# Depthwise convolution taps on VectorE: two operations per tap against one over three blocks of tokens

## The chip, the cores and the metric

The kernel runs on one core of one Trainium2 chip. The metric is device time in microseconds (us) of one execution. Three runs of the kernel before gave 1216.16, 1216.24 and 1216.39 us, median 1216.24. The profile shows one more execution.

## The reference

Two independent groups of tokens pass through two layers with shared weights: 128 context tokens and 256 latent tokens, 384 in all, each 1024 wide. A layer is a mixer part (pooling, two kinds of attention, a Fourier mix, gates, an output projection) and then the part that matters here, a gated MLP with a centred depthwise convolution of width 3 along the tokens of each group:

```
def _conv_ffn(h, w_up, conv_w, conv_b, w_down):
    u = h @ w_up                                   # 1024 -> 5632
    up = jnp.pad(u, ((0, 0), (1, 1), (0, 0)))
    u = up[:, :-2] * conv_w[0] + up[:, 1:-1] * conv_w[1] + up[:, 2:] * conv_w[2] + conv_b
    gate, val = jnp.split(u, 2, axis=-1)
    return (jax.nn.silu(gate) * val) @ w_down      # 2816 -> 1024
```

Every channel adds its left neighbour token times conv_w[0] and its right neighbour times conv_w[2]. Neighbours are taken inside a group alone: token 127 (last of the context) and token 128 (first of the latent group) are not neighbours.

## The kernel before, in words

Channels lie on the 128 partitions and the 384 tokens along the free axis, context in columns 0 to 127 and latent tokens in 128 to 383. `RANGES` is the pair of column ranges (0, 128) and (128, 384).

Weights stream from HBM in units of 128x1024 fp32, through four slots. Each unit is split in two parts: ScalarE copies it to fp32r (`w_hi<-w_raw`), VectorE subtracts that from the original (`w_lo<-w_raw,w_hi`, line 1077), and TensorE multiplies hi by hi, hi by lo and lo by hi (lines 1602 to 1604), 24 matmuls of 384 columns for a unit. TensorE starts a unit only when its w_hi and w_lo are both there (`unit_ready`, lines 1592 to 1595), and a slot is filled again only when TensorE has finished the unit that had it. In program order every engine has its own stream, and the engines meet in semaphores.

The up projection has 44 units in each layer, in pairs of a gate unit and a value unit. I call what VectorE and ScalarE do for one such pair a block: 22 blocks in a layer, numbered from 0. TensorE writes unit n to PSUM bank n modulo 4 in the first layer and modulo 8 in the second. For a block, with m = 0 for the gate and m = 1 for the value unit:

- ScalarE waits for both units, writes the middle tap with bias of each (`mlp_tmp<-bank,params` 128x384, lines 991 to 993), and signals `tap1` after each one.
- VectorE waits for `tap1` of m, adds the left neighbours (line 1492) and the right neighbours (line 1496), each as one operation per range, 127 and 255 columns, with a wait on its own semaphore between the two taps. That makes 8 operations a block. After m = 0 it signals `conv_g`, after m = 1 `conv_v`.
- ScalarE waits for `conv_g`, computes the tanh (`mlp_tmp<-mlp_tmp`), splits a weight unit, waits for `mlp_full`, and writes `mlp_hi`.
- VectorE forms the product (lines 1505 and 1508), splits a weight unit (line 1077), subtracts for `mlp_lo` (line 1080), and in the first layer and later blocks of the second does one row product (line 1108) for the modulation vectors of a later stage. Before the taps it splits another weight unit.

The first four blocks of the second layer differ, because there the up projection begins before the norm is known: VectorE scales the product in its bank (`bank<-bank,rstd`, line 1166, semaphore `rescaled`), ScalarE adds a shift to it in place (`bank<-bank,cond_raw`, 128 and 256 columns) ahead of each middle tap, and both also write normalised activations (`act_hi`, and `act_lo` at line 1144) for the units from 8 on. ScalarE waits there for VectorE's `rescaled` of m = 0 and of m = 1, and VectorE waits for ScalarE's `tap1`.

All ScalarE activations are recorded at line 673, a helper.

Of the kernel before, what the change touches and what calls it, by code (L numbers as in the profile page):

```python
# [19 lines left out]
ACT = mybir.ActivationFunctionType  # L20
ALU = mybir.AluOpType
AX = mybir.AxisListType.X

P = 128
# [5 lines left out]
TOK = CTX + LAT  # L30
# [8 lines left out]
FB = FFN // P  # L39
# [133 lines left out]
def program(nc, stream, start_w, ada_w, ada_rows, start_ada, params, caches, consts, time_consts, x_in, cond,  # L173
            y_out, k_out, v_out, ckv_out, krope_out):
    ctx = ExitStack()
    with ctx:
# [16 lines left out]
        late_t, _ = tile("gated_late", KD * TOK, o)  # L193
# [3 lines left out]
        for s in range(SLOTS):  # L197

            wlo.append(tile(f"w_lo{s}", UNIT, o, F32R)[0])
            t, o = tile(f"w_raw{s}", UNIT, o)  # L200
            raw.append(t)
            t, o = tile(f"w_hi{s}", UNIT, o, F32R)
# [141 lines left out]
        def pc(name, a=0, b=None, p0=0, p1=P):  # L344
            lo, hi = PCOL[name]
            return par[p0:p1, lo + a:(hi if b is None else lo + b)]
# [324 lines left out]
        def _(act):  # L671
            def A(out, in_, func, **kw):
                return nc.scalar.activation(out, in_, func, **kw)  # L673
# [22 lines left out]
            for l in range(DEPTH):  # L696
# [275 lines left out]
                for i in range(FB // 2):  # L972
                    for j in range(2):
                        u = P0 + 2 * j
                        p = l * FB + i * 2 + j
                        f = ftmp[:, j]
                        unnormed = l > 0 and i < 2
                        first, b0 = 3 * (2 * i + j), up_bank(i, 2 * j)
                        if unnormed and p > l * FB:
                            split(u + 4, i)  # L980
                        elif not unnormed and (l == 0 or i > 2 or j > 0):
                            split(u + 3, i)
                        act.wait_ge(unit_done, FROM + l * UNITS + i * SLOTS + u + 2)

                        act.wait_ge(mlp_lo, FROM + l * FB + i * 2 + j)
                        for m in range(2):
                            col = i * 4 + 2 * j + m
                            if unnormed:
                                add_shift(1, b0 + m, bank[b0 + m]).then_inc(shifted, 1)
                                act.wait_ge(shifted, b0 + m + 1)  # L990
                            A(f[:, m, :], bank[b0 + m][:, 0:TOK], ACT.Identity,
                              scale=pc("conv_w", 2 * FB + col, 2 * FB + col + 1),
                              bias=pc("conv_b", col, col + 1)).then_inc(tap1, 1)
                        if unnormed and p == l * FB:
                            split(u + 4, i)
                        if unnormed and first < KD:
                            normed_high(1, first)
                        act.wait_ge(conv_g, FROM + p + 2)
                        A(f[:, 2, :], f[:, 0, :], ACT.Tanh, scale=0.5).then_inc(mlp_tanh, 1)
                        if unnormed and first + 1 < KD:  # L1000
                            normed_high(1, first + 1)
                        split(u + (5 if unnormed else 4), i)
                        act.wait_ge(mlp_full, p + 1)
                        A(ghi[:, i * 2 + j, :], f[:, 3, :],
                          ACT.Copy).then_inc(mlp_hi, 1)
                        if unnormed and first + 2 < KD:
                            normed_high(1, first + 2)
# [27 lines left out]
        def _(dve):  # L1035
# [32 lines left out]
            for l in range(DEPTH):  # L1068
# [406 lines left out]
                for i in range(FB // 2):  # L1475
                    for j in range(2):
                        u = P0 + 2 * j
                        p = l * FB + i * 2 + j
                        f = ftmp[:, j]
                        unnormed = l > 0 and i < 2  # L1480
                        first, b0 = 3 * (2 * i + j), up_bank(i, 2 * j)
                        if unnormed and p > l * FB:
                            split(u + 4, i)
                        elif not unnormed and (l == 0 or i > 2 or j > 0):
                            split(u + 3, i)
                        for m in range(2):
                            dve.wait_ge(tap1, 2 * p + m + 1)
                            b = bank[b0 + m]
                            col = i * 4 + 2 * j + m
                            before, behind = pc("conv_w", col, col + 1), pc("conv_w", 4 * FB + col, 4 * FB + col + 1)  # L1490
                            for a, e, _ in RANGES:
                                own(V.scalar_tensor_tensor(f[:, m, a + 1:e], b[:, a:e - 1], before, f[:, m, a + 1:e],  # L1492
                                                           ALU.mult, ALU.add))
                            own.wait()
                            for a, e, _ in RANGES:
                                ins = V.scalar_tensor_tensor(f[:, m, a:e - 1], b[:, a + 1:e], behind, f[:, m, a:e - 1],  # L1496
                                                             ALU.mult, ALU.add)
                            ins.then_inc((conv_g, conv_v)[m], 1)
                        if unnormed and p == l * FB:
                            split(u + 4, i)  # L1500
                        if unnormed and first < KD:
                            normed_low(1, first)
                        dve.wait_ge(mlp_tanh, p + 1)

                        own(V.scalar_tensor_tensor(f[:, 2, :], f[:, 2, :], 1.0, f[:, 0, :], ALU.add, ALU.mult))
                        own.wait()
                        dve.wait_ge(conv_v, FROM + p + 2)
                        V.scalar_tensor_tensor(f[:, 3, :], f[:, 2, :], 0.5, f[:, 1, :], ALU.mult, ALU.mult).then_inc(mlp_full, 1)
                        if unnormed and first + 1 < KD:
                            normed_low(1, first + 1)  # L1510
                        split(u + (5 if unnormed else 4), i)
                        if unnormed and b0 < FIRST - 2:
                            rescale(1, b0 + 2, bank[b0 + 2][:, 0:TOK])
                        dve.wait_ge(mlp_hi, p + 1)
                        low(glo[:, i * 2 + j, :], f[:, 3, :],
                            ghi[:, i * 2 + j, :]).then_inc(mlp_lo, 1)
                        if unnormed and b0 < FIRST - 2:
                            rescale(1, b0 + 3, bank[b0 + 3][:, 0:TOK])
                        if unnormed and first + 2 < KD:
                            normed_low(1, first + 2)  # L1520
                        if l == 0 or i >= SLOW_ROWS:
                            dve.wait_ge(spread_loaded, 32 + 16 * l)
                            row_products(1, spread, prod_t)
# [664 lines left out]
```

## Time and profile before

| | |
|---|---|
| median of three runs | 1216.24 us |
| the profiled execution | 1215.3 us |
| its span, first to last instruction | 1213.5 us |
| granted TensorE clock | 1.00 throughout |
| busy: TensorE, VectorE, ScalarE, GpSimd | 99%, 78%, 50%, 12% |
| up projection and blocks, first layer | about 353 to 530 us of the span |
| the same, second layer | about 939 to 1127 us |
| line 1492, line 1496 | 64.7 and 65.2 us busy, 176 operations each |
| middle tap on ScalarE | 54.8 us busy, 88 operations |

A row of the timeline reads: start in us of the span, duration in us, engine, line, operation, what is written from what is read, shapes, how many like it were merged (xN), and in brackets how long the engine sat idle before it and what ended that. Where two operations with different numbers of columns are merged (127 and 255), the shape is that of the first. Rows of groups give the number of instructions, total busy time in us, the mean of one in ns, and the idle time before them.

### The profile page before, as it was taken

How to read it: one execution, taken by the hardware profiler on the slowest of the kernel's cores; microseconds unless marked ns; L12 is line 12 of the kernel's file. 1: busy time of each engine (PE TensorE's matmuls, PEld its weight loads, DVE VectorE, ACT ScalarE, POOL GpSimd, SP SyncE). 2: the span in 40 equal slices, each digit the busy share in tenths (PEclk: the TensorE clock that was granted, in tenths of full speed). 3: DMA queues.
4: the chain of work that ended last, by engine and by line, in shares of the span. 5: the costliest groups of instructions: out<-in, count | busy, mean ns of one | idle time of the engine just before them, and what ended most of it. 6: DMA issues, size and time to landing. Idle time of an engine off the chain costs nothing.

```text
span 1213.5 us, 19749 instructions
## 1 busy us (share of the span) xinstructions
PE 1200.7 (99%) x7688; PEld 1146.9 (95%) x7688; DVE 946.2 (78%) x1751; ACT 601.5 (50%) x1023; POOL 149.8 (12%) x125
## 2 busy tenths in 40 slices
PE   8999999999999999999999999999999999999998
PEld 7987999989989999999999889999999999999998
DVE  5587877848689999988867978787687899999432
ACT  3445564543365544543456555646438755454221
POOL 0232000008300000000142500000272200000000
PEclk9999999999999999999999999999999999999999
DMA  9763433544744454457663544343325444454443
GB/s 371 293 223 124 142 119 121 172 142 157 260 175 140 162 168 156 161 197 244 218 249 122 208 139 140 105 133 111 105 87 196 140 134 139 158 167 145 139 139 122
DMA packets 53821, 200.91 MB, mean 166 GB/s; under 512 B 6816, under 2 KB 7232, under 8 KB 51936
## 3 DMA queue, kind: packets, MB, share of 16 engines
q1 hardware_dynamic: 53408, 198.96, 47.9%
q8 instruction: 62, 1.02, 0.3%
q0 software_dynamic: 320, 0.69, 0.2%
q14 instruction: 31, 0.25, 0.1%
HBM read 197.35 MB, written 2.27 MB: 164 GB/s over the span
## 4 chain that ended last, share of the span: by engine, by line
PE 95%; DVE 2%; DMA 1%; issue 1%; SPq 0%; ACT 0%; DVEq 0%
PE bank L1602 28%; PE bank L1604 27%; PE bank L1603 27%; PE bank L1920 1%; PE bank L1900 1%; DMA start_ada<-start_ada 1%; DVE w_lo L1077 1%; PE bank L1669 1%; PE bank L1674 1%; PE bank L1890 1%; PE bank L1673 1%; DVE gated_late L1431 1%; PE bank L1875 1%; PE bank L1658 1%; PE bank L1724 0%
## 5 line engine op out<-in xcount | busy, mean ns | idle before, releaser
L1602 PE MATMUL bank<-act_hi,w_hi 128*128 128x384 f32 x1240 | 421.9, 340 | 0.1
L1604 PE MATMUL bank<-act_hi,w_lo 128*128 128x384 f32 x1240 | 415.0, 335 | 0.0
L1603 PE MATMUL bank<-act_lo,w_hi 128*128 128x384 f32 x1208 | 403.9, 334 | 0.0
L1077 DVE TENSOR_TENSOR w_lo<-w_raw,w_hi 128x1024 fp32r<-128x1024 f32 x251 | 323.5, 1291 | 98.0 <-ACT w_hi L673 97.3
L673 ACT ACTIVATE w_hi<-w_raw 128x1024 fp32r<-128x1024 f32 x251 | 264.1, 1053 | 153.4 <-DMA w_raw<-stream 153.3
L1602 PEld LDWEIGHTS bank<-act_hi,w_hi 128*128 128x128 f32 x1240 | 233.1, 188 | 8.7 <-issue 5.3
L1604 PEld LDWEIGHTS bank<-act_hi,w_lo 128*128 128x128 f32 x1240 | 232.8, 188 | 0.0
L1603 PEld LDWEIGHTS bank<-act_lo,w_hi 128*128 128x128 f32 x1208 | 227.0, 188 | 0.6
L1604 PE MATMUL bank<-mlp_hi,w_lo 128*128 128x384 f32 x352 | 118.3, 336 | 0.0
L1602 PE MATMUL bank<-mlp_hi,w_hi 128*128 128x384 f32 x352 | 118.3, 336 | 0.0
L1603 PE MATMUL bank<-mlp_lo,w_hi 128*128 128x384 f32 x352 | 118.3, 336 | 0.0
L673 ACT ACTIVATE mlp_tmp<-bank,params 128x384 f32<-128x384 f32 x88 | 54.8, 668 | 73.3 <-PE bank L1604 73.1
L1492 DVE SCALAR_TENSOR_TENSOR mlp_tmp<-bank,params,mlp_tmp 128x127 f32<-128x127 f32 (+1 forms) x176 | 64.7, 409 | 16.0 <-ACT mlp_tmp L673 16.0
L1496 DVE SCALAR_TENSOR_TENSOR mlp_tmp<-bank,params,mlp_tmp 128x127 f32<-128x127 f32 (+1 forms) x176 | 65.2, 412 | 3.1
L1604 PEld LDWEIGHTS bank<-mlp_hi,w_lo 128*128 128x128 f32 x352 | 66.2, 188 | 0.0
L1602 PEld LDWEIGHTS bank<-mlp_hi,w_hi 128*128 128x128 f32 x352 | 66.2, 188 | 0.0
L1603 PEld LDWEIGHTS bank<-mlp_lo,w_hi 128*128 128x128 f32 x352 | 66.2, 188 | 0.0
L1108 DVE SCALAR_TENSOR_TENSOR row_products_mix<-ada,cond_spread_mix 128x1024 f32<-128x1024 f32 x44 | 55.7, 1267 | 4.9 <-DMA cond_spread_mix<-cond_rows 2.3
L673 ACT ACTIVATE gates_b<-bank 128x384 f32<-128x384 f32 x48 | 23.6, 492 | 63.9 <-PE bank L1604 63.6
L1363 DVE TENSOR_REDUCE small<-bank 128x1 f32<-128x384 f32 (+1 forms) x72 | 31.3, 463 | 28.2 <-PE bank L1878 11.1
L662 POOL TENSOR_TENSOR wide<-wide 128x768 f32<-128x768 f32 x8 | 18.7, 2344 | 273.9 <-DVE wide L1431 273.9
L673 ACT ACTIVATE mlp_tmp<-mlp_tmp 128x384 f32<-128x384 f32 x44 | 23.1, 525 | 46.9 <-DVE mlp_tmp L1496 46.9
(261 smaller groups left out, 1891.5 us busy)
## 6 DMA issues: line engine op xcount, KB each, us to landing
w_raw<-stream SPq DMA_DIRECT2D x251, 512.0 KB, 3.7
ada<-ada_rows SPq DMA_DIRECT2D x64, 512.0 KB, 4.6
start_ada<-start_ada SPq DMA_DIRECT2D x8, 1024.0 KB, 17.8
ada<-ada_w SPq DMA_DIRECT2D x8, 512.0 KB, 5.4
ada_norm<-ada_w SPq DMA_DIRECT2D x8, 512.0 KB, 5.8
start_raw<-start_w SPq DMA_DIRECT2D x8, 448.0 KB, 18.4
cond_spread_mix<-cond_rows SPq DMA_DIRECT2D x2, 1024.0 KB, 8.2
cond_spread<-cond_rows SPq DMA_DIRECT2D x2, 1024.0 KB, 8.3
```

Source lines behind the costliest of these rows:

```text
L662: own(nc.gpsimd.tensor_tensor(g[:, 0:2, :], g[:, 0:2, :], g[:, 2:4, :], ALU.add))
L673: return nc.scalar.activation(out, in_, func, **kw)
L1077: V.tensor_tensor(wlo[s][:, :], raw[s][:, :], whi[s][:, :].bitcast(F32), ALU.subtract).then_inc(lo_ready, 1)
L1108: V.scalar_tensor_tensor(out[:, :], ada[b % 2][:, :], 1.0, tile[:, t, :], ALU.mult, ALU.mult, accum_out=mod[:, at, t:t + 1]).then_inc(rows ...
L1363: own(V.reduce_max(small[:, c + m:c + m + 1], bank[score_bank(i, m)][:, 0:n], AX))
L1431: V.scalar_tensor_tensor(gated[d % GATED][:, n, :], gates[n * KD + d], 1.0, bank[branch_bank[4 * d + n]][:, 0:TOK], ALU.add, ALU.mult).the ...
L1492: own(V.scalar_tensor_tensor(f[:, m, a + 1:e], b[:, a:e - 1], before, f[:, m, a + 1:e], ALU.mult, ALU.add))
L1496: ins = V.scalar_tensor_tensor(f[:, m, a:e - 1], b[:, a + 1:e], behind, f[:, m, a:e - 1], ALU.mult, ALU.add)
L1602: T.matmul(out, wb[s][0][:, w, :], hi[k], start=first and k == 0, stop=False)
L1603: T.matmul(out, wb[s][0][:, w, :], lo[k], start=False, stop=False)
L1604: ins = T.matmul(out, wb[s][1][:, w, :], hi[k], start=False, stop=last and k == n - 1)
L1658: ins = T.matmul(bank[7][p0:p0 + STRIP, j * n:(j + 1) * n], conds[:, k, :], w[:, c:c + n], start=k == 0, stop=k == KD - 1)
```

## The change

Each tap on VectorE becomes one operation over three blocks of 128 tokens, each block with 127 columns (381 in all) instead of one of 127 and one of 255. The latent group spans two of these blocks, so its columns 255 and 256 lack one neighbour each. ScalarE adds these: after both middle taps, four operations on a single column, each a multiply by a per-partition weight and an add of a per-partition value, reading the bank in PSUM. `tap1` of m is now signalled after the two single columns of m, so both middle taps stand ahead of the first signal. `own.wait(1 - m)` makes ScalarE wait until its own middle tap of m is written.

```
-                            A(f[:, m, :], bank[b0 + m][:, 0:TOK], ACT.Identity,
-                              scale=pc("conv_w", 2 * FB + col, 2 * FB + col + 1),
-                              bias=pc("conv_b", col, col + 1)).then_inc(tap1, 1)
+                            own(A(f[:, m, :], bank[b0 + m][:, 0:TOK], ACT.Identity,
+                                  scale=pc("conv_w", 2 * FB + col, 2 * FB + col + 1),
+                                  bias=pc("conv_b", col, col + 1)))
+                        for m in range(2):
+                            col = i * 4 + 2 * j + m
+                            own.wait(1 - m)
+                            A(f[:, m, 2 * P:2 * P + 1], bank[b0 + m][:, 2 * P - 1:2 * P], ACT.Identity,
+                              scale=pc("conv_w", col, col + 1), bias=f[:, m, 2 * P:2 * P + 1])
+                            A(f[:, m, 2 * P - 1:2 * P], bank[b0 + m][:, 2 * P:2 * P + 1], ACT.Identity,
+                              scale=pc("conv_w", 4 * FB + col, 4 * FB + col + 1),
+                              bias=f[:, m, 2 * P - 1:2 * P]).then_inc(tap1, 1)
...
-                            for a, e, _ in RANGES:
-                                own(V.scalar_tensor_tensor(f[:, m, a + 1:e], b[:, a:e - 1], before, f[:, m, a + 1:e],
-                                                           ALU.mult, ALU.add))
+                            fm = f[:, m, :].rearrange("p (t c) -> p t c", c=P)
+                            bm = b[:, 0:TOK].rearrange("p (t c) -> p t c", c=P)
+                            own(V.scalar_tensor_tensor(fm[:, :, 1:P], bm[:, :, 0:P - 1], before, fm[:, :, 1:P],
+                                                       ALU.mult, ALU.add))
                             own.wait()
-                            for a, e, _ in RANGES:
-                                ins = V.scalar_tensor_tensor(f[:, m, a:e - 1], b[:, a + 1:e], behind, f[:, m, a:e - 1],
-                                                             ALU.mult, ALU.add)
-                            ins.then_inc((conv_g, conv_v)[m], 1)
+                            V.scalar_tensor_tensor(fm[:, :, 0:P - 1], bm[:, :, 1:P], behind, fm[:, :, 0:P - 1],
+                                                   ALU.mult, ALU.add).then_inc((conv_g, conv_v)[m], 1)
```

ScalarE's stream before, in block 3 of the second layer (the last with a shift added in the bank):

```order
L673 ACTIVATE bank<-bank,cond_raw 128x128 [waits rescaled,mlp_lo,unit_done]
L673 ACTIVATE bank<-bank,cond_raw 128x256
L673 ACTIVATE mlp_tmp<-bank,params 128x384 [waits shifted]
L673 ACTIVATE bank<-bank,cond_raw 128x128 [waits rescaled]
L673 ACTIVATE bank<-bank,cond_raw 128x256
L673 ACTIVATE mlp_tmp<-bank,params 128x384 [waits shifted]
L673 ACTIVATE mlp_tmp<-mlp_tmp 128x384 [waits conv_gate]
```

The same place of ScalarE's stream now:

```order
L673 ACTIVATE bank<-bank,cond_raw 128x128 [waits rescaled,mlp_lo,unit_done]
L673 ACTIVATE bank<-bank,cond_raw 128x256
L673 ACTIVATE mlp_tmp<-bank,params 128x384 [waits shifted]
L673 ACTIVATE bank<-bank,cond_raw 128x128 [waits rescaled]
L673 ACTIVATE bank<-bank,cond_raw 128x256
L673 ACTIVATE mlp_tmp<-bank,params 128x384 [waits shifted]
L673 ACTIVATE mlp_tmp<-bank,mlp_tmp,params 128x1 [waits act_own]
L673 ACTIVATE mlp_tmp<-bank,mlp_tmp,params 128x1
L673 ACTIVATE mlp_tmp<-bank,mlp_tmp,params 128x1 [waits act_own]
L673 ACTIVATE mlp_tmp<-bank,mlp_tmp,params 128x1
L673 ACTIVATE mlp_tmp<-mlp_tmp 128x384 [waits conv_gate]
```

Four single-column operations stand between the second middle tap and the tanh, and the first signal to VectorE comes after the second of them instead of after the first middle tap.

VectorE's stream before, in block 3 of the second layer:

```order
L1492 SCALAR_TENSOR_TENSOR mlp_tmp<-bank,params,mlp_tmp 128x127 [waits tap1]
L1492 SCALAR_TENSOR_TENSOR mlp_tmp<-bank,params,mlp_tmp 128x255
L1496 SCALAR_TENSOR_TENSOR mlp_tmp<-bank,params,mlp_tmp 128x127 [waits dve_own]
L1496 SCALAR_TENSOR_TENSOR mlp_tmp<-bank,params,mlp_tmp 128x255
L1492 SCALAR_TENSOR_TENSOR mlp_tmp<-bank,params,mlp_tmp 128x127 [waits tap1]
L1492 SCALAR_TENSOR_TENSOR mlp_tmp<-bank,params,mlp_tmp 128x255
L1496 SCALAR_TENSOR_TENSOR mlp_tmp<-bank,params,mlp_tmp 128x127 [waits dve_own]
L1496 SCALAR_TENSOR_TENSOR mlp_tmp<-bank,params,mlp_tmp 128x255
L1505 SCALAR_TENSOR_TENSOR mlp_tmp<-mlp_tmp 128x384 [waits mlp_tanh]
```

The same place of VectorE's stream now:

```order
L1501 SCALAR_TENSOR_TENSOR mlp_tmp<-bank,params,mlp_tmp 128x3x127 [waits tap1]
L1504 SCALAR_TENSOR_TENSOR mlp_tmp<-bank,params,mlp_tmp 128x3x127 [waits dve_own]
L1501 SCALAR_TENSOR_TENSOR mlp_tmp<-bank,params,mlp_tmp 128x3x127 [waits tap1]
L1504 SCALAR_TENSOR_TENSOR mlp_tmp<-bank,params,mlp_tmp 128x3x127 [waits dve_own]
L1512 SCALAR_TENSOR_TENSOR mlp_tmp<-mlp_tmp 128x384 [waits mlp_tanh]
```

Eight operations became four; the waits stand where they stood. Over the program ScalarE has 176 operations more and VectorE 176 fewer. TensorE's, GpSimd's and the DMA queue's streams are the same.

## Rows read from the trace of the kernel before

**Rows 1.** The page: span, and the first line of busy time.

```profile
span 1213.5 us, 19749 instructions
PE 1200.7 (99%) x7688; PEld 1146.9 (95%) x7688; DVE 946.2 (78%) x1751; ACT 601.5 (50%) x1023; POOL 149.8 (12%) x125
```

**Rows 2.** TensorE's waits: who waited for whom, total us, times, longest.

```profile
PE bank L1602 <- DVE w_lo L1077: 1.9, 2, 1.1
```

**Rows 3.** Stretches: busy us and instructions by engine, granted clock, DMA share, GB/s.

```profile
440.00:520.00 80.00, 80.00 (x464) 80.00 (x463) 74.69 (x143) 40.43 (x58) 0.00 (x0) 1.00 0.49 159
1140.00:1200.00 60.00, 60.00 (x348) 60.00 (x347) 22.24 (x26) 15.91 (x15) 0.00 (x0) 1.00 0.47 147
```

**Rows 4.** Groups by shape, VectorE: taps, and the like with 384 columns.

```profile
L1492 DVE SCALAR_TENSOR_TENSOR mlp_tmp<-bank,params,mlp_tmp 128x255 f32<-128x255 f32 x88 | 41.7, 474 | 0.0
...
L1492 DVE SCALAR_TENSOR_TENSOR mlp_tmp<-bank,params,mlp_tmp 128x127 f32<-128x127 f32 x88 | 30.3, 344 | 16.0 <-ACT mlp_tmp L673 16.0
...
L1330 DVE SCALAR_TENSOR_TENSOR mla_k<-mla_k,params,bank 96x384 f32<-96x384 f32 x8 | 4.4, 607 | 7.6 <-PE bank L1825 7.6
```

**Rows 5.** Groups by shape, ScalarE: middle tap, plain copies, a one-column operation.

```profile
L673 ACT ACTIVATE mlp_tmp<-bank,params 128x384 f32<-128x384 f32 x88 | 54.8, 668 | 73.3 <-PE bank L1604 73.1
...
L673 ACT ACTIVATE gates_b<-bank 128x384 f32<-128x384 f32 x48 | 23.6, 492 | 63.9 <-PE bank L1604 63.6
...
L673 ACT ACTIVATION_READ_ACCUMULATOR wide<-bank,small 128x1 f32 x72 | 14.8, 205 | 0.0
...
L673 ACT ACTIVATE proj<-bank 128x128 f32<-128x128 f32 x8 | 2.2, 271 | 0.0
```

**Rows 6.** Timeline of ScalarE, VectorE and TensorE, first layer, block 0.

```profile
354.06 1.24 ACT L673 ACTIVATE mlp_tmp<-bank,params 128x384 f32<-128x384 f32 x2 [0.32 <-PE bank L1604]
...
354.92 0.74 DVE L1492 SCALAR_TENSOR_TENSOR mlp_tmp<-bank,params,mlp_tmp 128x127 f32<-128x127 f32 x2
...
357.77 0.55 DVE L1505 SCALAR_TENSOR_TENSOR mlp_tmp<-mlp_tmp 128x384 f32<-128x384 f32 x1
...
358.83 1.22 DVE L1077 TENSOR_TENSOR w_lo<-w_raw,w_hi 128x1024 fp32r<-128x1024 f32 x1
...
360.19 0.41 PE L1602 MATMUL bank<-act_hi,w_hi 128*128 128x384 f32 x1
```

**Rows 7.** Timeline of ScalarE, second layer, blocks 0, 1, 3 and 4.

```profile
945.68 0.67 ACT L673 ACTIVATE mlp_tmp<-bank,params 128x384 f32<-128x384 f32 x1
...
955.37 0.67 ACT L673 ACTIVATE mlp_tmp<-bank,params 128x384 f32<-128x384 f32 x1
...
974.74 0.67 ACT L673 ACTIVATE mlp_tmp<-bank,params 128x384 f32<-128x384 f32 x1
...
979.08 1.22 ACT L673 ACTIVATE mlp_tmp<-bank,params 128x384 f32<-128x384 f32 x2
```

**Rows 8.** Timeline of VectorE, second layer, blocks 0, 1, 3 and 4.

```profile
945.08 0.74 DVE L1492 SCALAR_TENSOR_TENSOR mlp_tmp<-bank,params,mlp_tmp 128x127 f32<-128x127 f32 x2 [0.75 <-ACT mlp_tmp L673]
...
955.91 0.74 DVE L1492 SCALAR_TENSOR_TENSOR mlp_tmp<-bank,params,mlp_tmp 128x127 f32<-128x127 f32 x2
...
974.63 0.73 DVE L1492 SCALAR_TENSOR_TENSOR mlp_tmp<-bank,params,mlp_tmp 128x127 f32<-128x127 f32 x2
...
980.14 0.73 DVE L1492 SCALAR_TENSOR_TENSOR mlp_tmp<-bank,params,mlp_tmp 128x127 f32<-128x127 f32 x2
...
984.05 1.22 DVE L1077 TENSOR_TENSOR w_lo<-w_raw,w_hi 128x1024 fp32r<-128x1024 f32 x1
```

**Rows 9.** Timeline of TensorE, second layer, first matmul of unit 12.

```profile
985.64 0.33 PE L1602 MATMUL bank<-act_hi,w_hi 128*128 128x384 f32 x1
```

**Rows 10.** Timeline of ScalarE, VectorE and TensorE, second layer, block 20.

```profile
1110.64 1.24 ACT L673 ACTIVATE mlp_tmp<-bank,params 128x384 f32<-128x384 f32 x2 [2.10 <-PE bank L1604]
...
1115.26 1.22 DVE L1077 TENSOR_TENSOR w_lo<-w_raw,w_hi 128x1024 fp32r<-128x1024 f32 x1
...
1118.76 0.33 PE L1602 MATMUL bank<-mlp_hi,w_hi 128*128 128x384 f32 x1
```

## The prediction, made before the result was known

> **What bounds the kernel.** I read the page first: TensorE is busy 1200.7 of 1213.5 us [rows 1], so a change on VectorE and ScalarE pays only where TensorE waits for them, and costs only where it makes TensorE wait. TensorE's waits come next: the only ones put down to VectorE are 1.9 us for w_lo ahead of line 1602 [rows 2], both in the merge of the mixer, which the change doesn't touch. Then the stretches: in the up projection TensorE is busy 80.00 of 80.00 us [rows 3]. The 24 or so microseconds of VectorE time that go away therefore buy nothing by themselves. What is left to read is the margin: how long before TensorE starts a unit its w_lo is ready, and where that margin is smallest. The timelines of the engines, side by side, show it:
>
> - First layer, block 0: w_lo of unit 4 ends at 358.83 + 1.22 = 360.05, and the unit's first matmul starts at 360.19 [rows 6]. It lasts 0.41 us where another first matmul lasts 0.33 [rows 9], so the pipeline had run empty: the margin is nil, and 0.14 us is the lead that a start needs.
> - Second layer, block 4: w_lo of unit 12 ends at 984.05 + 1.22 = 985.27 [rows 8], and the unit starts at 985.64 [rows 9]. With the lead of 0.14 the margin is 0.23 us.
> - Steady state, block 20: w_lo ends at 1116.48 and the unit starts at 1118.76 [rows 10], a margin of 2.1 us. ScalarE idles 2.10 us before the taps.
>
> **VectorE's part.** From the first tap to line 1505 it takes 357.77 - 354.92 = 2.85 us [rows 6]. That is four pairs of 344 and 474 ns [rows 4]; a pair lasts 0.74 [rows 6], 0.08 less than the two singly, since neighbours overlap. Two pairs are followed by a wait on VectorE's own semaphore and cost 0.74 + 0.03 each, two cost 0.66, together 2.86. The slope is (474 - 344) / 128 = 1.02 ns a column, so 381 columns cost 607 - 3 = 604 ns by the row of the same kind of operation (a per-partition scalar, one operand in PSUM, 384 columns) [rows 4]. New: 2 x (0.604 + 0.03) + 2 x (0.604 - 0.08) = 2.32 us. A block saves 0.53 us. Bounds of the merged operation, whose three-block shape no row shows: 474 ns (the part of 255 alone) and 818 ns (both parts in full); I take 604.
>
> **ScalarE's part.** No row shows a one-column operation with two per-partition operands from PSUM. A plain copy from PSUM costs 492 ns for 384 columns and 271 for 128, 0.86 ns a column; the middle tap costs 668 [rows 5]. One column is then 668 - 383 x 0.86 = 339 ns, and since the two middle taps last 1.24 together [rows 6] rather than 2 x 0.668, neighbours overlap by 0.10: 0.57 us from tap to tap, 0.24 from one small operation to the next. Bounds: 205 ns with 0.10 from start to start (the one-column operation that has a row [rows 5]) and 668 with 0.57 (a whole tap). I take 0.34 and 0.24.
>
> Here the price per operand can be weighed. The trace has 668 against 492 for two operands more, 88 ns each [rows 5]. The Trainium skill, "ScalarE: Activation LUTs", on what an ACTIVATE costs, gives 186 ns + 0.833 ns a column, about 93 ns more for each pointer operand, and an overlap of about 93 ns between neighbours. The trace agrees on the operand and on the overlap. By the page one column would be 373 ns, 280 from start to start; with that the sum below would be 0.4 us larger, about 1219.2 us.
>
> More than their length, their place counts. The first signal to VectorE used to come at the end of the first middle tap. Now it comes after the second tap's slot (0.57), one slot of a small operation (0.24) and the end of another (0.34), and 0.03 for the signal: 1.18 us after the second tap's start. Where VectorE waits for it, everything behind it on VectorE is late: both taps, the product, the w_lo splits, mlp_lo. TensorE waits for the splits.
>
> **The path, second layer.** "Late" is against the time before. In blocks 0 to 3 ScalarE's additions in the bank wait for VectorE's rescaling, so a late VectorE makes ScalarE equally late.
>
> - Block 0: the signal comes at 945.68 + 1.18 = 946.86 [rows 7], VectorE started at 945.08 [rows 8]: 1.78 of waiting, less 0.53: 1.25 late.
> - Block 1: 955.37 + 1.18 [rows 7] against 955.91 [rows 8]: 0.64, less 0.53: 1.36 late.
> - Block 2 repeats block 1 9.69 us on: 1.47 late.
> - Block 3: 974.74 + 1.18 [rows 7] against 974.63 [rows 8]: 1.29, less 0.53: 2.23 late.
> - Block 4: the second tap starts at 979.08 + 0.57 [rows 7], behind mlp_hi of block 3, which is as late as VectorE; + 1.18 against 980.14 [rows 8]: 0.69, less 0.53: 2.39 late.
>
> w_lo of unit 12 stands behind block 4's product, so 2.39 late; less the margin of 0.23, TensorE loses 2.16 us. Units 9 and 11 would be held up by less and lie before it, so they are not added. Nothing behind it returns the loss: TensorE has no gap in the rest of the up projection, nor in the down projection [rows 3].
>
> **The path, first layer.** Block 0: second tap at 354.06 + 0.57, signal at 355.81 against 354.92 [rows 6]: 0.89, less 0.53: 0.36 late, at a margin of nil: 0.36 us lost. From block 1 on, ScalarE is ahead and VectorE only gains.
>
> **Steady state.** ScalarE adds 4 x 0.24 = 0.96 us to a block and has 2.10 idle; VectorE waits about 1.05 more and saves 0.53, so it is 0.5 late against a margin of 2.1 [rows 10]: nothing. With that cover gone it would cost up to 0.5 us once in each layer, not once a block, since each block starts anew from TensorE. The last block's mlp_lo has a like margin.
>
> **Sum.** 2.16 + 0.36 = 2.5 us. The profiled execution had a span of 1213.5 us and 1215.3 in all, 0.9 below the median of 1216.24 of the runs; it would become 1217.8, and the median 1218.8.
>
> **Rivals.**
>
> - *The small operations are nearly free.* At 0.205 and 0.10 each of six waits is 0.27 us shorter, 1.6 in all: a loss of 0.9, 1217.1 us. A merged operation nearer to 474 would save up to 0.5 more in each of six places and leave no loss, 1216.2. For it: the row of 205. Against it: that row has no operand to fetch.
> - *The three-block shape costs as the pieces did.* 818 instead of 604 ns is 0.86 us a block, and with six blocks on the two paths 5.1 more: 7.7, 1223.9 us. Then steady VectorE time rises instead of falling. Against it: the fixed part, 344 - 127 x 1.02 = 214 ns, belongs to an instruction, as the row of 607 shows.
> - *Faster, by less contention.* If VectorE's accesses slow TensorE, removing a tenth of them in the up projection returns time. A matmul takes 80 / 464 = 0.172 us [rows 3], 12 ns over the 160 that 384 columns take at the granted 2.4 GHz. Over the 2112 matmuls of both up projections that is 25 us, and a tenth of it 2.5: with the forecast loss it comes out even, and with the loss gone at 1213.7 us. It is measurably faster only where the loss is under 0.1 us. Against it: TensorE ran 464 matmuls in 80 us (5.80 a us) with VectorE 93% busy, and 348 in 60 (5.80) with it 37% busy [rows 3].
> - *The change does not do what it says*: the merged operation is split again, or nothing is saved. Then the sum is 2.5 + 6 x 0.53 = 5.7, 1221.9 us; I count it with the second.
>
> **How the numbers follow.** A measurement of this kernel tells about 0.2%, 2.4 us, from no change: slower begins at 1218.67. The forecast case (1217.8 to 1220.0) has 0.63, split at that line 0.41 to 0.22. The small operations nearly free: 0.22, all within 0.2%. The shape expensive or nothing saved: 0.10, slower. Contention: 0.05, faster. So slower 0.51, same 0.44, faster 0.05. The range of 8 in 10 leaves out the contention case, the top of the second rival and a little of the first: 1216.7 to 1221.2 us.
>
> **What would show it.** Right: taps of about 604 ns, x88 for each of the two lines; small operations of about 0.34 us; VectorE's wait for ScalarE ahead of the taps up from 16.0 us to about 50; TensorE idle about 2.1 us ahead of unit 12 of the second layer, with w_lo named, and 0.3 to 0.4 us longer than before ahead of unit 4 of the first; all else unmoved. Wrong: no wait of TensorE near 986 us (small operations cheaper), waits at units 7 and 9 already (dearer), or another matmul rate in the up projection.

## The result and the profile after

The changed kernel took 1218.60 us, median of 9 runs (1218.33 to 1222.35); the kernel before took 1216.06 us, median of 9 (1215.02 to 1216.75). The ratio is 1.0025, interval 1.0017 to 1.0034. The forecast was 1218.8 us. The profiled execution of the changed kernel took 1219.96 us, 1.4 above its median, with a span of 1218.1 us; below it turns out where that 1.4 lies.

The page after, its span and first line of busy time:

```profile
span 1218.1 us, 19749 instructions
PE 1201.7 (99%) x7688; PEld 1147.0 (94%) x7688; DVE 925.8 (76%) x1575; ACT 643.3 (53%) x1199; POOL 148.6 (12%) x125
```

Against [rows 1] VectorE lost 20.4 us of work (24 or so was predicted) in 176 operations fewer, ScalarE gained 41.8 us in 176 more, and TensorE is busy for the same time within 1.0 us in a span 4.6 longer. The groups by shape, after (columns as in [rows 4]):

```profile
L1501 DVE SCALAR_TENSOR_TENSOR mlp_tmp<-bank,params,mlp_tmp 128x381 f32<-128x381 f32 x88 | 53.6, 609 | 41.4 <-ACT mlp_tmp L673 41.4
L1504 DVE SCALAR_TENSOR_TENSOR mlp_tmp<-bank,params,mlp_tmp 128x381 f32<-128x381 f32 x88 | 54.1, 615 | 3.1
L673 ACT ACTIVATE mlp_tmp<-bank,params 128x384 f32<-128x384 f32 x88 | 54.7, 667 | 56.6 <-PE bank L1611 56.3
L673 ACT ACTIVATE mlp_tmp<-bank,mlp_tmp,params 128x1 f32<-128x1 f32 x176 | 47.4, 359 | 0.0
```

The merged tap takes 609 and 615 ns, near the 607 of a flat operation of 384 columns [rows 4]. A single-column operation takes 359 ns. TensorE's waits, after, where [rows 2] had 1.9 us in two:

```profile
PE bank L1609 <- DVE w_lo L1085: 3.9, 5, 1.3
...
PE bank L1731 <- ACT proj L673: 1.2, 1, 1.2
PE bank L1750 <- ACT rstd L673: 1.1, 1, 1.1
```

The first row is the change at work: three waits for w_lo more, the longest 1.3 us. The second row stands at 655 us and was 1.1 us before; the third, at 669 us, is new, and is taken up below. The table of waits puts down only what lies between two matmuls' ends and starts, so the sizes are better read from the starts of the same matmul in both programs. The timeline of TensorE after, at the four units (the first answers to [rows 6], the last to [rows 9]):

```profile
360.69 0.41 PE L1609 MATMUL bank<-act_hi,w_hi 128*128 128x384 f32 x1 [0.32 <-DVE w_lo L1085]
...
975.93 0.41 PE L1609 MATMUL bank<-act_hi,w_hi 128*128 128x384 f32 x1 [0.41 <-DVE w_lo L1085]
...
984.45 0.41 PE L1609 MATMUL bank<-act_hi,w_hi 128*128 128x384 f32 x1
...
990.14 0.41 PE L1609 MATMUL bank<-act_hi,w_hi 128*128 128x384 f32 x1 [1.26 <-DVE w_lo L1085]
```

The two in the middle are units 9 and 11. TensorE's timeline before has them here:

```profile
973.16 0.33 PE L1602 MATMUL bank<-act_hi,w_hi 128*128 128x384 f32 x1
...
981.48 0.33 PE L1602 MATMUL bank<-act_hi,w_hi 128*128 128x384 f32 x1
```

"Behind" below means a matmul's start after less its start before, each counted from the start of its span. I took it for all 7688 matmuls of the program in order, and noted by how much it grows from one place to the next (places by the time of the kernel before). A second profiled execution of the same changed kernel (label again, span 1216.9 us) is read in the same way:

| where | first execution | second |
|---|---|---|
| start of the program | +0.16 | +0.35 |
| from there to unit 4 | -0.05 | -0.01 |
| unit 4, first layer | +0.39 | +0.39 |
| 655 us | +0.12 | +0.17 |
| 669 us, TensorE waits for ScalarE's rstd | +1.18 | none |
| 916 us | +0.38 | +0.05 |
| unit 9, second layer | +0.67 | +0.67 |
| unit 11 | +0.19 | +0.19 |
| unit 12 | +1.53 | +1.53 |
| sum, which is the difference of the spans | 4.57 | 3.34 |

Unit 4 and the three units of the second layer repeat within 0.01 us; together they are 2.78 us in both. The 1.18 does not repeat, nor does most of the 0.38; they lie in stages that the change doesn't touch, and they cover the 1.4 us by which the first execution lay above its median. One execution's span was no measure of this change; its gaps were.

The 1.18 us has a cause that the traces show. ScalarE forms rstd, for which TensorE waits, right behind a weight split, and the split waits for its weights to land. ScalarE before, then after:

```profile
666.64 1.06 ACT L673 ACTIVATE w_hi<-w_raw 128x1024 fp32r<-128x1024 f32 x1 [1.78 <-DMA w_raw<-stream]
```

```profile
669.12 1.06 ACT L673 ACTIVATE w_hi<-w_raw 128x1024 fp32r<-128x1024 f32 x1 [3.65 <-DMA w_raw<-stream]
```

The other profiled executions bear it out. In four of the eleven ScalarE waits 1.6 to 2.2 us for these weights and TensorE has no stall here (the kernel before, again, in_turn and twice); in the other seven it waits 2.6 to 3.6 us and TensorE stalls for 0.1 to 1.1 us, the longer the later the weights. So a transfer of weights lands late in some executions and not in others. Why it does is not shown.

Where the lateness comes from is seen on the timelines. VectorE after, second layer, blocks 0, 1, 3 and 4, and the splits of units 9, 11 and 12, as [rows 8]:

```profile
949.05 0.61 DVE L1501 SCALAR_TENSOR_TENSOR mlp_tmp<-bank,params,mlp_tmp 128x381 f32<-128x381 f32 x1 [2.53 <-ACT mlp_tmp L673]
...
960.02 0.61 DVE L1501 SCALAR_TENSOR_TENSOR mlp_tmp<-bank,params,mlp_tmp 128x381 f32<-128x381 f32 x1 [0.56 <-ACT mlp_tmp L673]
...
974.57 1.22 DVE L1085 TENSOR_TENSOR w_lo<-w_raw,w_hi 128x1024 fp32r<-128x1024 f32 x1
...
979.67 0.61 DVE L1501 SCALAR_TENSOR_TENSOR mlp_tmp<-bank,params,mlp_tmp 128x381 f32<-128x381 f32 x1 [1.22 <-ACT mlp_tmp L673]
...
983.08 1.22 DVE L1085 TENSOR_TENSOR w_lo<-w_raw,w_hi 128x1024 fp32r<-128x1024 f32 x1
...
985.36 0.61 DVE L1501 SCALAR_TENSOR_TENSOR mlp_tmp<-bank,params,mlp_tmp 128x381 f32<-128x381 f32 x1 [0.60 <-ACT mlp_tmp L673]
...
988.77 1.22 DVE L1085 TENSOR_TENSOR w_lo<-w_raw,w_hi 128x1024 fp32r<-128x1024 f32 x1
```

ScalarE after, block 0, and the two middle taps of block 4, as [rows 7]:

```profile
947.86 0.67 ACT L673 ACTIVATE mlp_tmp<-bank,params 128x384 f32<-128x384 f32 x1
948.44 1.07 ACT L673 ACTIVATE mlp_tmp<-bank,mlp_tmp,params 128x1 f32<-128x1 f32 x4
...
983.63 1.22 ACT L673 ACTIVATE mlp_tmp<-bank,params 128x384 f32<-128x384 f32 x2
```

In block 0 the second middle tap starts at 947.86, the four single columns take 1.07 us behind it, and VectorE, which has waited 2.53 us, starts at 949.05, as the second of them ends. Before, VectorE started 0.60 us ahead of that second tap [rows 7, 8].

### The profile page after: what moved, and what is told of

Read it like the earlier page. It is cut to its first block, busy times and chain, and to the rows that moved or that the text cites. A ratio compares the mean times of both kernels' runs of the same rounds, so it can differ in the third digit from the quotient of the medians.

```text
span 1218.1 us, 19749 instructions
## 1 busy us (share of the span) xinstructions
PE 1201.7 (99%) x7688; PEld 1147.0 (94%) x7688; DVE 925.8 (76%) x1575; ACT 643.3 (53%) x1199; POOL 148.6 (12%) x125
## 3 DMA queue, kind: packets, MB, share of 16 engines
q8 instruction: 62, 1.02, 0.3%
## 4 chain that ended last, share of the span: by engine, by line
PE 89%; DVE 4%; ACT 2%; DMA 2%; issue 2%; SPq 0%; DVEq 0%; ACTq 0%
PE bank L1609 25%; PE bank L1610 25%; PE bank L1611 25%; PE bank L1927 1%; PE bank L1907 1%; DVE w_lo L1085 1%; DMA w_raw<-stream 1%; PE bank L1676 1%; ACT mlp_tmp L673 1%; DMA start_ada<-start_ada 1%; PE bank L1681 1%; PE bank L1680 1%; PE bank L1897 1%; DVE mlp_tmp L1504 1%; PE bank L1665 1%
## 5 line engine op out<-in xcount | busy, mean ns | idle before, releaser
L1501 DVE SCALAR_TENSOR_TENSOR mlp_tmp<-bank,params,mlp_tmp 128x381 f32<-128x381 f32 x88 | 53.6, 609 | 41.4 <-ACT mlp_tmp L673 41.4
L1504 DVE SCALAR_TENSOR_TENSOR mlp_tmp<-bank,params,mlp_tmp 128x381 f32<-128x381 f32 x88 | 54.1, 615 | 3.1
L673 ACT ACTIVATE mlp_tmp<-bank,mlp_tmp,params 128x1 f32<-128x1 f32 x176 | 47.4, 359 | 0.0
```

The source lines that it names most:

```text
L1501: own(V.scalar_tensor_tensor(fm[:, :, 1:P], bm[:, :, 0:P - 1], before, fm[:, :, 1:P], ALU.mult, ALU.add))
L1504: V.scalar_tensor_tensor(fm[:, :, 0:P - 1], bm[:, :, 1:P], behind, fm[:, :, 0:P - 1], ALU.mult, ALU.add).then_inc((conv_g, conv_v)[m], 1)
```

## The experiments

Expectations speak of the kernels by their labels. In the code, `...` stands for arguments or lines that are left out. A ratio is against runs of the kernel before on the same chip. The kernel before had medians of 1215.86 us (33 runs), 1215.88 (16) and 1215.74 (15) beside them.

**again**: the changed kernel unaltered.

> The changed kernel unaltered, for its profile a second time. In the first profile its span is 4.6 us over that of before, but the medians are only 2.5 apart. Theory: of the 4.6, TensorE's late starts at unit 4 of the first layer (0.40) and units 9, 11 and 12 of the second (0.58, 0.11, 1.43) belong to the change and come again to within 0.05; the 1.18 us more at 671 us (TensorE on ScalarE's rstd, in the mixer of the second layer) and 0.38 at 918 us do not come again. Rival: the 1.18 at 671 us is caused by the change too and is there again. Time 1218.6, 2.5 over before.

1218.81 us, ratio 1.0023 (1.0015 to 1.0032). The loss is real, and its places are those of the table. TensorE's first matmuls of units 4, 9, 11 and 12 are later by 0.39, 0.59, 0.11 and 1.43 us, as expected within 0.01; the table also counts the matmuls just behind them, up to 0.1 us more. The 1.18 us at 669 us is not there.

**no_cols**: the single columns are left out.

```
-                            own(A(f[:, m, :], ...
-                        for m in range(2):
-                            own.wait(1 - m)
-                            A(f[:, m, 2 * P:2 * P + 1], ...
-                            A(f[:, m, 2 * P - 1:2 * P], ...
+                            A(f[:, m, :], bank[b0 + m][:, 0:TOK], ACT.Identity, ...).then_inc(tap1, 1)
```

> Leaves out the four single columns of each block (columns 255 and 256 of the latent tokens lack one neighbour each), with the signals of before: one tap, one signal. VectorE's merged taps alone. Theory: VectorE is early by 0.5 us a block and TensorE had nothing of it to wait for but 0.1 us: 1216.0 to 1216.1, within 0.2 of before; no wait at units 9, 11, 12. Rival, less contention: 2.5 us faster than before, 1213.6. Rival, the merged taps themselves are what costs: 1217 or more.

1215.90 us, ratio 1.0000 (0.9992 to 1.0009). No stall is left at units 9, 11 and 12. This is VectorE's half of the change alone, with its 20 us less of work: it costs nothing and gives nothing that the time shows (unit 4 of the first layer, where the margin was nil, goes on 0.17 us earlier). The contention rival, which had 1213.6, and the rival of the dear shape, which had 818 ns a tap, both fall here. The groups by shape of this kernel:

```profile
L1493 DVE SCALAR_TENSOR_TENSOR mlp_tmp<-bank,params,mlp_tmp 128x381 f32<-128x381 f32 x88 | 53.6, 609 | 36.7 <-ACT mlp_tmp L673 36.7
```

VectorE saves 20 us and waits 20.7 longer than in [rows 4]: the work that went turned into waiting.

**in_turn**: all the work of the change, but the columns of m directly behind the middle tap of m.

```
                             own(A(f[:, m, :], ...))          # middle tap of m
-                        for m in range(2):
-                            own.wait(1 - m)
+                            own.wait()
                             A(f[:, m, 2 * P:2 * P + 1], ...)
                             A(f[:, m, 2 * P - 1:2 * P], ...).then_inc(tap1, 1)
```

> The changed kernel with ScalarE's order altered: the two single columns of m = 0 come right after the middle tap of m = 0, and its signal before the middle tap of m = 1. All the work is there. Theory (the place of the first signal costs, not the work): the first signal comes 1.34 us after its tap's start and the second 1.3 to 1.9 later; late by 0.9, 0.6, 0.4, 0.75, 0.5 in blocks 0 to 4 of the second layer, so 0.3 us lost at unit 12 and nothing in the first layer: 1216.4. Rival (the work of 0.96 us a block on ScalarE costs): still 1218 or more.

1216.20 us, ratio 1.0004 (0.9995 to 1.0013). The same 176 operations on ScalarE and the same taps on VectorE, and 2.6 us of the 2.95 are gone. TensorE's waits, then VectorE's first taps of block 0 on the timeline:

```profile
PE bank L1607 <- DVE w_lo L1083: 2.1, 3, 1.1
```

```profile
945.92 0.61 DVE L1499 SCALAR_TENSOR_TENSOR mlp_tmp<-bank,params,mlp_tmp 128x381 f32<-128x381 f32 x1 [1.38 <-ACT mlp_tmp L673]
...
947.85 0.61 DVE L1499 SCALAR_TENSOR_TENSOR mlp_tmp<-bank,params,mlp_tmp 128x381 f32<-128x381 f32 x1 [0.67 <-ACT mlp_tmp L673]
```

The first wait is 1.38 instead of 2.53, because the first signal no longer stands behind the shift and the middle tap of the second unit. The second tap waits 0.67 more, so not all is won back: TensorE still loses 0.41 us at unit 12, and nothing at units 4, 9 and 11.

**unit12_early**: the changed kernel with unit 12's split, on ScalarE and VectorE, ahead of block 4's taps instead of behind its product; nothing is put in its old place. The edit stands twice, once for each engine:

```
+                        elif l > 0 and i == 2:
+                            split(u + 4, i)
...
-                        split(u + (5 if unnormed else 4), i)
+                        if not (l > 0 and i == 2 and j == 0):
+                            split(u + (5 if unnormed else 4), i)
```

> The changed kernel with one weight split moved: in block 4 of the second layer ScalarE and VectorE split unit 12 ahead of the taps instead of behind the product. Theory (TensorE loses only what w_lo of a unit is late against its margin): the wait at unit 12 is gone, those at units 9 and 11 (0.6 and 0.1) and at unit 4 of the first layer (0.4) stay: 1.1 us over before, 1217.2. Rival (the block as a whole has become the pace): the wait moves to unit 13 or 14 and the time stays 1218.6.

1217.92 us, ratio 1.0017 (1.0008 to 1.0026); 2.06 us above before, where 1.1 was expected: a miss. The stall at unit 12 is gone as expected, but one of 0.80 us appears at unit 14, as the rival had it; the rival's time of 1218.6 does not come. TensorE at unit 14, then VectorE's timeline, which shows why:

```profile
996.37 0.41 PE L1615 MATMUL bank<-act_hi,w_hi 128*128 128x384 f32 x1 [0.56 <-DVE w_lo L1088]
```

```profile
989.04 0.56 DVE L1091 TENSOR_TENSOR mlp_lo<-mlp_tmp,mlp_hi 128x384 fp32r<-128x384 f32 x1 [0.59 <-ACT mlp_hi L673]
...
989.99 1.23 DVE L1088 TENSOR_TENSOR w_lo<-w_raw,w_hi 128x1024 fp32r<-128x1024 f32 x1 [0.39 <-ACT w_hi L673]
```

With no split between the product and mlp_lo, VectorE waits 0.59 us for ScalarE's mlp_hi and then 0.39 for w_hi. The split behind the product was work, and also what filled the time of a round trip to ScalarE.

**one_ahead**: the same idea without the hole. Blocks 4 and 5 split one unit further ahead: 12 before the taps of block 4, 13 behind its product, 14 behind the product of block 5. This edit, too, stands once for each engine:

```
-                        elif not unnormed and (l == 0 or i > 2 or j > 0):
+                        elif not unnormed and (l == 0 or i > 2):
                             split(u + 3, i)
+                        elif l > 0 and i == 2 and j == 0:
+                            split(u + 4, i)
...
-                        split(u + (5 if unnormed else 4), i)
+                        split(u + (5 if unnormed or (l > 0 and i == 2 and j == 0) else 4), i)
```

> The changed kernel with the splits of blocks 4 and 5 of the second layer one unit ahead: unit 12 before block 4's taps, 13 behind its product, 14 behind block 5's. Unlike the run that moved unit 12 alone, a split still stands between product and mlp_lo on VectorE and covers ScalarE's mlp_hi. Theory: units 9 and 11 hold TensorE up by 0.7 together, unit 4 of the first layer by 0.4, units 12 to 14 not at all: 1.1 over before, 1217.0. Rival (VectorE is late as a whole and any order loses it): 2.0 over or more, with a wait at units 13 or 14.

1217.23 us, ratio 1.0010 (1.0001 to 1.0019). It is 1.35 us above before, where 1.1 was expected. Nothing is left at units 12 to 14; units 9 and 11 keep about 0.7 and 0.2, unit 4 of the first layer 0.4. Margin where the lateness arrives is as good as no lateness, but for what is already lost at units 9 and 11.

**late_signal**: the kernel before, with only the signals moved: both come with the end of the second middle tap. No operation is added, none merged.

```
+                            ins = A(f[:, m, :], bank[b0 + m][:, 0:TOK], ACT.Identity, ...)
+                            if m == 1:
+                                ins.then_inc(tap1, 2)
```

> The kernel before with one thing altered: both signals to VectorE come at the end of the second middle tap. No single columns, no merged taps. Theory (the place of the first signal is the mechanism): it comes 0.70 us after the second tap's start, so waits of 1.30, 0.16, 0.16, 0.81 and 0.21 in blocks 0 to 4 of the second layer, 2.6 late against a margin of 0.23: 2.4 lost, and 0.41 in the first layer: 2.8 us over before, 1218.7. Rival (the added operations are the cause): same as before.

1219.43 us, ratio 1.0030 (1.0018 to 1.0041): 3.5 us from a signal's place alone, in a kernel whose work is that of before. The forecast was 2.8. VectorE's waits for it are 2.10 and 0.80 us in blocks 0 and 3:

```profile
947.21 0.74 DVE L1494 SCALAR_TENSOR_TENSOR mlp_tmp<-bank,params,mlp_tmp 128x127 f32<-128x127 f32 x2 [2.10 <-ACT mlp_tmp L673]
...
978.10 0.74 DVE L1494 SCALAR_TENSOR_TENSOR mlp_tmp<-bank,params,mlp_tmp 128x127 f32<-128x127 f32 x2 [0.80 <-ACT mlp_tmp L673]
```

TensorE loses 2.76 us in the second layer and 0.42 at unit 4 of the first. That makes 3.2; the profiled execution has 0.47 more at 669 us, outside the change. The forecast lacked 0.4 of the 3.2. VectorE's taps of blocks 0 to 4 come later, one block after the other, by 1.36, 0.22, 0.23, 0.89 and 0.21 us where 1.30, 0.16, 0.16, 0.81 and 0.21 were forecast, 0.27 together, and the slower first matmul of unit 12 adds 0.08.

**old_taps**: ScalarE as in the change, VectorE's eight operations as before, so that the 0.5 us of a block are not saved. Against the changed kernel VectorE's two merged operations go, and the pairs come back:

```
+                            for a, e, _ in RANGES:
+                                own(V.scalar_tensor_tensor(f[:, m, a + 1:e], b[:, a:e - 1], before, ...))
                             own.wait()
+                            for a, e, _ in RANGES:
+                                ins = V.scalar_tensor_tensor(f[:, m, a:e - 1], b[:, a + 1:e], behind, ...)
```

> ScalarE as in the changed kernel, VectorE's taps as before (eight operations a block, both neighbours of columns 255 and 256 added by them as well, so these columns get one neighbour twice). The other half of the change alone. Theory: each block on the two paths loses the 0.53 us that the merged taps saved, one in the first layer and five in the second: 2.5 + 6 x 0.53 = 5.7 us over before, 1221.5, with TensorE held up at unit 4 of the first layer by 0.9 and at units 7 to 12 of the second by 4.8 together. Rival (the single columns cost by themselves, VectorE's time does not matter): 2.5 over, as the changed kernel.

1221.86 us, ratio 1.0053 (1.0041 to 1.0066). Without the cheaper taps the loss doubles, from 2.95 to 5.98 us: six places times 0.5.

This run and late_signal take the change apart. With VectorE's work as it was, the signal's new place alone costs 3.55 us; the single columns that also stand ahead of it cost 2.4 more (5.98 - 3.55; by the gaps of the two profiled executions, 5.90 - 3.18, it is 2.7); and the merged taps give back 3.0.

**twice**: two more single-column operations, into a buffer that nobody reads, ahead of each pair.

```
+                            for c in range(2):
+                                A(rt_t[:, 500 + 2 * m + c:501 + 2 * m + c], bank[b0 + m][:, c:c + 1], ...)
```

> The changed kernel with two more one-column operations (same kind, into unused space) ahead of the two of each m, so eight a block instead of four, and both signals later by two slots or more. Theory: each wait on the two paths grows by 2 x 0.24 = 0.48 us, six of them: 2.9 more than the changed kernel, 5.4 over before, 1221.3; in the steady state nothing, since ScalarE still has about 0.2 us idle and w_lo a margin of 1 us. Rival (a fixed cost of the new form of wait, not the work): 2.5 over.

1221.75 us, ratio 1.0049 (1.0036 to 1.0061): 2.94 us over again, where 2.9 more was expected. The price of a single column in place is read from VectorE's waits, blocks 0 and 4:

```profile
948.19 0.61 DVE L1504 SCALAR_TENSOR_TENSOR mlp_tmp<-bank,params,mlp_tmp 128x381 f32<-128x381 f32 x1 [3.02 <-ACT mlp_tmp L673]
...
986.48 0.61 DVE L1504 SCALAR_TENSOR_TENSOR mlp_tmp<-bank,params,mlp_tmp 128x381 f32<-128x381 f32 x1 [1.08 <-ACT mlp_tmp L673]
```

Two operations more ahead of the first signal make it 3.02 - 2.53 = 0.49 and 1.08 - 0.60 = 0.48 us later: 0.24 us each. TensorE's wait at unit 12 is 1.78 here, and a new one of 0.94 us appears for act_lo near 975 us.

**turn_ahead**: in_turn and one_ahead together, all the work of the change done.

> Both cures together, all the work done: ScalarE's single columns of m = 0 right after its middle tap (as in in_turn), and the splits of blocks 4 and 5 of the second layer one unit ahead (as in one_ahead). Theory: the 0.35 us that in_turn still lost at unit 12 goes, TensorE waits nowhere in either up projection but where it did before: 1215.9, not to be told from before, since TensorE has nothing left there to gain. Rival, less contention: 1 us or more faster than before.

1215.74 us, ratio 1.0000 (0.9991 to 1.0009), TensorE's waits for w_lo back at those of [rows 2]:

```profile
PE bank L1611 <- DVE w_lo L1085: 1.9, 2, 1.1
```

The loss is undone entirely. It is not turned into a gain, since TensorE has no wait left in the up projection that VectorE or ScalarE could shorten.

## Why the prediction was right

- **TensorE bounds, the saved VectorE time buys nothing.** Shown by no_cols (1215.90 against 1215.86) and turn_ahead.
- **VectorE's part.** 604 ns forecast, 609 and 615 measured. From the first tap to the product in block 0 of the first layer it is 358.27 - 355.92 = 2.35 us against 2.32: a block saves 0.50, not 0.53.

```profile
354.17 1.23 ACT L673 ACTIVATE mlp_tmp<-bank,params 128x384 f32<-128x384 f32 x2 [0.31 <-PE bank L1611]
355.29 1.08 ACT L673 ACTIVATE mlp_tmp<-bank,mlp_tmp,params 128x1 f32<-128x1 f32 x4
...
355.92 0.61 DVE L1501 SCALAR_TENSOR_TENSOR mlp_tmp<-bank,params,mlp_tmp 128x381 f32<-128x381 f32 x1 [0.80 <-ACT mlp_tmp L673]
...
358.27 0.55 DVE L1512 SCALAR_TENSOR_TENSOR mlp_tmp<-mlp_tmp 128x384 f32<-128x384 f32 x1
...
359.33 1.22 DVE L1085 TENSOR_TENSOR w_lo<-w_raw,w_hi 128x1024 fp32r<-128x1024 f32 x1
```

- **ScalarE's part.** 0.34 us long and 0.24 from start to start forecast. The length is 0.36; the distance is 0.24, from four in 1.07 us ((1.07 - 0.36) / 3) and from twice. By an estimate from the figures of the Trainium skill, "ScalarE: Activation LUTs", section "What ACT_TABLE_LOAD costs", they are 373 ns and 280: nearer in the length, not in the distance. The path pays for both, the distance once for each operation ahead and the length for the last.
- **The place of the signal.** 1.18 us after the second tap's start forecast, 949.05 - 947.86 = 1.19 measured. late_signal and in_turn show that the place of the signal, and not the 42 us of added work as such, makes the loss: in in_turn all the work stays and 2.6 of the 2.95 us go, and in late_signal no work is added and 3.5 us are lost. The added work does cost where it stands ahead of the signal (old_taps, twice).
- **The path, second layer.** When block 0 starts the program is 2.18 us behind for other reasons (947.86 against 945.68 [rows 7]). Less that, VectorE's taps of block 4 start 985.36 - 980.14 - 2.18 = 3.04 later than before [rows 8]; less the saving of 0.50 it is 2.54 late, forecast 2.39. The 0.15 is the saving, 0.03 less in each of five blocks. Less the margin of 0.23 that is 2.31. On top comes what I hadn't counted: a unit whose weights come too late starts with a matmul of 0.41 us instead of 0.33, 0.08 us. 2.39 in all, as in the table (0.67 + 0.19 + 1.53), against 2.16.
- **The path, first layer.** 0.36 forecast, 0.39 measured in both executions; the 0.03 is the saving again.
- **Steady state.** Half a microsecond late at a margin of 2.1, forecast; block 20's w_lo starts at 1120.38, 5.12 later than in [rows 10], of which 4.57 are the program's: 0.55, and TensorE loses nothing there.

```profile
1115.21 1.23 ACT L673 ACTIVATE mlp_tmp<-bank,params 128x384 f32<-128x384 f32 x2 [1.57 <-PE bank L1611]
...
1116.96 0.61 DVE L1501 SCALAR_TENSOR_TENSOR mlp_tmp<-bank,params,mlp_tmp 128x381 f32<-128x381 f32 x1 [0.94 <-ACT mlp_tmp L673]
...
1120.38 1.22 DVE L1085 TENSOR_TENSOR w_lo<-w_raw,w_hi 128x1024 fp32r<-128x1024 f32 x1
```

- **The sum, and some luck.** The forecast was 2.16 + 0.36 = 2.52 us, the gaps are 2.39 + 0.39 = 2.78. The 0.26 between them are the saving, 0.03 too large in each of six blocks, and the 0.08. The medians are 2.54 us apart in the result and 2.95 in again, and the interval of the first is 2.1 to 4.1 us, so that 1218.60 came within 0.2 us of 1218.8 is closer than such a measurement can promise. The prediction's own line between same and slower, 1218.67, runs through the middle of this: the result lies just below it, again just above.

Two marks under "what would show it" were wrong, though the sum was not:

- **"TensorE idle about 2.1 us ahead of unit 12".** It is 1.26 there, with 0.41 ahead of unit 9 and a gap too short to be listed ahead of unit 11. The prediction said that 9 and 11 lie before it and aren't added, and then put the whole loss at unit 12. It should have read their margins. Before, w_lo of unit 9 was ready 0.97 us ahead of need and that of unit 11 1.58 (their splits on VectorE before are shown below; 973.16 and 981.48 less the lead of 0.14, less the ends of the splits); with the lateness of 1.47 and 2.23 that is 0.50 at unit 9 and 0.65 by unit 11, and only 1.5 would be left for unit 12. The total is set by the worst place, since an earlier stall is time that the later one no longer needs; where it shows is set by all of them. A reader who held to that mark would have taken the wait at unit 9 for a sign of dearer operations.

```profile
970.83 1.22 DVE L1077 TENSOR_TENSOR w_lo<-w_raw,w_hi 128x1024 fp32r<-128x1024 f32 x1
...
978.54 1.22 DVE L1077 TENSOR_TENSOR w_lo<-w_raw,w_hi 128x1024 fp32r<-128x1024 f32 x1
```

- **VectorE's wait ahead of the taps, 16.0 to about 50.** It is 41.4. I added 1.05 us a block, but a block's VectorE also ends its work before the taps 0.5 later than it did, so the wait grows only by what is saved: 0.94 in block 20, and 0.43 in the kernel before. A wait grows by the difference of two delays, not by one.

Not settled: why the weights ahead of 669 us land late in some executions, and why smaller steps at 655 and 916 come and go. At 669 us six of the other kernels lose 0.2 to 0.8 us, no_cols among them, and two lose nothing; the changed kernel itself lost 1.18 once and nothing the second time. So it is not the change's doing.

## What to carry to other kernels

Before work is added to an engine with time to spare, look at where its next signal stands: operations of 0.24 us cost 0.3 us behind the signal's own tap, and nothing once the next splits had margin (turn_ahead), while the same ones cost 2.95 us when both signals stood behind the neighbour's tap as well, because the engine that waits for them has other work in line for the bounding engine. Read the margin of every unit near a change of regime and not of the steady state alone (2.1 us there, 0.23 at the one that decided), and compute the loss as the largest of lateness less margin, over the units. Then move work from the units that have no margin to those that have it, but look at what the moved work had covered (unit12_early).

## What the runs showed of the hardware

- VectorE's access pattern of three blocks of 127 columns with gaps costs 609 to 615 ns, about what a flat one of 384 does (607, or 604 for 381 by the slope of 1.02 ns a column): the gaps cost 5 to 11 ns, a second instruction far more (two of 127 and 255 columns take 344 + 474 ns).
- A one-column ScalarE operation from PSUM with two per-partition operands lasts 359 ns but delays the next only 0.24 us. Behind its own middle tap, whose end it must wait for, it is another matter: in_turn's timeline has 0.71 us from tap to column where two taps without a wait are 0.57 apart.

```profile
974.02 0.67 ACT L673 ACTIVATE mlp_tmp<-bank,params 128x384 f32<-128x384 f32 x1
974.73 0.59 ACT L673 ACTIVATE mlp_tmp<-bank,mlp_tmp,params 128x1 f32<-128x1 f32 x2
```
